# V and K in eight steps of two K tiles instead of four quarters, with the modulation weights in a new order

## What is computed

```python
m = silu(c) @ w_ada + b_ada                    # 9 vectors c; six parts of 2048: shift, scale, gate, twice
h = rms_norm(x, g_pre) * (1.0 + scale) + shift
z = h @ w_in                                   # 2048 -> 4096, columns q | k | v | u
q, k = rotary(q), rotary(k)                    # then differential attention, pooling, output, MLP
```

## Time and profile before

| what | value |
|---|---|
| median of 3 runs | 1501.66 us (1497.08 to 1504.21) |
| the profiled execution | 1498.26 us |
| its span, first to last instruction | 1496.6 us |
| PE busy | 1443.1 us (96%) |
| DVE busy | 798.9 us (53%) |
| ACT busy | 516.9 us (35%) |
| POOL busy | 102.5 us (7%) |
| mean granted TensorE clock | 0.995 |
| moved by DMA | 316.40 MB |

### The profile page before, as it was taken

One profiled execution on the slowest core, in us unless ns is written; L12 is line 12 of the kernel. 1 busy time (PEld: TensorE's weight loads), 2 busy tenths in 40 slices (PEclk: granted clock), 3 DMA queues, 4 the chain that ended last, 5 costly groups with the idle time before them and its releaser, 6 DMA issues.

```text
span 1496.6 us, 26948 instructions
## 1 busy us (share of the span) xinstructions
PE 1443.1 (96%) x10264; PEld 1313.5 (88%) x10264; DVE 798.9 (53%) x1258; ACT 516.9 (35%) x732; POOL 102.5 (7%) x177
## 2 busy tenths in 40 slices
PE   5999999999899998999999999999999999999996
PEld 1677777778688877999998999999999999999996
DVE  2555558846756568665434444334555344445554
ACT  2222244333356445333232333322333332333331
POOL 1000000067410000000000000000000000000002
PEclk9999999999999999999999999999999999999998
DMA  9999988889677787445445544445544444444431
GB/s 367 341 322 325 322 306 311 284 310 347 245 296 251 257 280 240 155 140 168 140 147 199 189 147 162 141 159 184 195 157 147 151 158 141 141 154 154 141 113 71
DMA packets 87880, 316.40 MB, mean 211 GB/s; under 512 B 12176, under 2 KB 12432, under 8 KB 87168
## 3 DMA queue, kind: packets, MB, share of 16 engines
q1 hardware_dynamic: 79200, 287.87, 55.9%
q0 software_dynamic: 5216, 22.51, 4.0%
q10 hardware_dynamic: 3392, 5.01, 1.0%
HBM read 309.56 MB, written 5.80 MB: 211 GB/s over the span
## 4 chain that ended last, share of the span: by engine, by line
PE 83%; DVE 5%; DMA 5%; POOL 2%; ACT 2%; issue 2%; POOLq 1%; SPq 0%; DVEq 0%; ACTq 0%
PE bank L1519 69%; PE bank L1583 7%; DMA raw<-in_stream 3%; PE bank L1481 3%; PE bank L1496 2%; DMA k_pages<-in_kc 1%; DVE w_lo L774 1%; DMA pools_out<-u_s 1%; POOL win L1382 1%; ACT w_hi L389 0%; ACT pair L631 0%; DVE back L978 0%; POOLq L1363 0%; DVE pair L1184 0%; ACT h_hi L635 0%
## 5 line engine op out<-in xcount | busy, mean ns | idle before, releaser
L774 DVE TENSOR_TENSOR w_lo<-raw,w_hi 128x1024 fp32r<-128x1024 f32 x352 | 419.6, 1225 | 121.7 <-ACT w_hi L389 119.8
L389 ACT ACTIVATE w_hi<-raw 128x1024 fp32r<-128x1024 f32 x352 | 361.6, 1054 | 355.9 <-PE bank L1519 232.8
L1519 PE MATMUL bank<-m_hi,w_hi 128*128 128x320 f32 x1280 | 397.4, 310 | 0.6 <-issue 0.6
L1519 PE MATMUL bank<-m_hi,w_lo 128*128 128x320 f32 x1280 | 395.5, 309 | 0.0
L1519 PE MATMUL bank<-m_lo,w_hi 128*128 128x320 f32 x1280 | 395.5, 309 | 0.0
L1519 PE MATMUL bank<-h_hi,w_hi 128*128 128x320 f32 x1216 | 379.2, 312 | 0.0
L1519 PE MATMUL bank<-h_hi,w_lo 128*128 128x320 f32 x1216 | 375.7, 309 | 0.0
L1519 PE MATMUL bank<-h_lo,w_hi 128*128 128x320 f32 x1216 | 375.6, 309 | 0.0
L1519 PEld LDWEIGHTS bank<-m_hi,w_hi 128*128 128x128 f32 x1280 | 240.3, 188 | 14.6 <-issue 14.6
L1519 PEld LDWEIGHTS bank<-h_hi,w_hi 128*128 128x128 f32 x1216 | 228.2, 188 | 24.1 <-issue 24.1
L1519 PEld LDWEIGHTS bank<-m_lo,w_hi 128*128 128x128 f32 x1280 | 240.3, 188 | 0.0
(11 more groups left out here) (234 smaller groups left out, 1093.8 us busy)
## 6 DMA issues: line engine op xcount, KB each, us to landing
raw<-in_stream SPq DMA_DIRECT2D x544, 512.0 KB, 4.9
k_pages<-in_kc POOLq DMA_DIRECT2D x16, 512.0 KB, 9.2
v_pages<-in_vc POOLq DMA_DIRECT2D x16, 512.0 KB, 7.3
x<-in_x_cm ACTq DMA_DIRECT2D x1, 2560.0 KB, 12.1
x<-in_x_cm POOLq DMA_DIRECT2D x1, 2560.0 KB, 11.3
v_out<-v_cm POOLq DMA_DIRECT2D x1, 1280.0 KB, 9.7
k_out<-back POOLq DMA_DIRECT2D x1, 1280.0 KB, 9.8
y_out<-x SPq DMA_DIRECT2D x2, 640.0 KB, 3.0
```

The costliest lines, as they stand in the source:

```text
L389: act.activation(w_hi[2 * (j % 2) + h][:, :], raw[slot][:, h * 1024:(h + 1) * 1024], ACT.Copy).then_inc(hi_ready, 1)
L774: dve.tensor_tensor(w_lo[q][:, :], raw[slot][:, h * 1024:(h + 1) * 1024], w_hi[q][:, :], ALU.subtract).then_inc(slot_used[slot], 1)
L1519: last = pe.matmul(bank[j % 2][:, 0:T], w[q][:, k * P:(k + 1) * P], v[:, 8 * h + k, :], start=(h == 0 and k == 0 and n == 0), stop=(h == 1 ...
```

## The change

**Steps.** V and K are made in eight steps (`SLICES`) of two K tiles. A product chunk now has eight column tiles by two K tiles: one chunk for V and one for K a step. A half has four column tiles, one in each of the four banks, six matmuls each, so a bank comes round once a half. The products stand at places 0, 3, 6, 9 of the 12 (`SLICED`). The number of chunks, of product matmuls and of modulation matmuls is the same; DVE adds 128 tiles of partial sums instead of 64.

**Modulation.** Block n (0 to 7) now has both scale and shift of two K tiles (`MOD_TILES`), so the first product needs block 0 alone: the head has four modulation chunks instead of eight. Block n+1 comes during step n. The prompt's scale and shift are one ACT instruction a K tile (`slice_h`, Identity with scale and bias); POOL's two operations are half as wide.

**Head.** x comes on SP's queue in four pieces ahead of the stream. PE sums the squares before block 0. DVE makes `normed` for eight K tiles before block 0 is added up.

**Q stage.** The four chunks that the head lost are here: 28 chunks, products at 0, 4, 7, 11, 14, 18, 21, 25 (`Q_PLACES`), 20 modulation chunks before a product or in its middle (`Q_BEFORE`, `Q_MIDDLE`).

```diff
-STREAM = 8 + 12 * QUARTERS + 12 * Q_GROUPS + 8 * (U_GROUPS + OUT_GROUPS) + 36 * GROUPS
-DENSE = [2, 5, 8, 11]
-DENSE_ADA = [[0, 1, 3, 4], [6, 7, 9, 10]]
+SLICES = 2 * QUARTERS
+STREAM = 4 + 12 * QUARTERS + 28 + 8 * (U_GROUPS + OUT_GROUPS) + 36 * GROUPS
+SLICED = [0, 3, 6, 9]
+SLICED_ADA = [[1, 2, 4, 5], [7, 8, 10, 11]]
+Q_PLACES = [0, 4, 7, 11, 14, 18, 21, 25]
+Q_ADA = [n for n in range(28) if n not in Q_PLACES]
+Q_BEFORE = [[0, 1, 2], [4], [6, 7], [9], [11], [13, 14], [16, 17], [19]]
+Q_MIDDLE = [[3], [5], [8], [10], [12], [15], [18], []]
+Q_TURN = {0: 9, 2: 10, 4: 11}
+NORMED = [(0, 2), (2, 4), (4, 8), (8, 12), (12, 16)]
...
     @block.sync
     def _(sp):
+        for g in range(4):
+            sp.dma_start(x[:, 4 * g:4 * g + 4, :], x_cm[:, 4 * g:4 * g + 4, :]).then_inc(x_loaded[g], 16)
...
     @block.scalar
-        act.dma_start(x[:, :, :], x_cm).then_inc(x_loaded, 16)
...
+        def slice_h(n):
+            act.wait_ge(gate_done, n + 1)
+            act.wait_ge(normed_s, normed_by(n))
+            act.wait_ge(mod_done, n + 2)
+            for k in range(2):
+                tile = normed[:, 2 * n + k, 0:NP_]
+                act.activation(tile, tile, ACT.Identity, bias=mod[:, n, 2 + k, 0:1], scale=gate[:, 2 * n + k, 0:1]).then_inc(
+                    prompt_mod, 1)
+            act.wait_ge(prompt_mod, 2 * n + 2)
+            act.wait_ge(sample_mod, n + 1)
+            act.activation(h_hi[:, 2 * n:2 * n + 2, :], normed[:, 2 * n:2 * n + 2, :], ACT.Copy).then_inc(h_hi_s, 1)
+
         ada_copy(0, 0, 3)
-        ada_copy(1, 1, 3)
+        hi_half(0, quarter_use(0), SLICED[0], 0, 0)
+        slice_h(0)
+        hi_half(0, quarter_use(0), SLICED[0], 0, 1)
...
+        for n in range(SLICES):
+            second, following = slice_chunks(n)
+            for h in range(2):
+                hi_half(*second, h)
+            ada_copy(n + 1, quarter_use(n // 2), SLICED_ADA[n % 2][3])
+            hi_half(*following, 0)
+            if n + 1 < SLICES:
+                slice_h(n + 1)
+            hi_half(*following, 1)
...
     @block.vector
+        def slice_gate(n):
+            mod_add(n)
+            dve.wait_ge(mod_done, n + 2)
+            dve.scalar_tensor_tensor(gate[:, 2 * n:2 * n + 2, :], mod[:, n, 0:2, :], 1.0,
+                                     gain[:, G_PRE_MIX + 2 * n:G_PRE_MIX + 2 * n + 2].unsqueeze(2).to_broadcast([P, 2, NSEQ]),
                                      ALU.add, ALU.mult).then_inc(gate_done, 1)
...
+        invert_root(0)
+        for first, end in NORMED[:3]:
+            times_rstd(first, end)
+        slice_gate(0)
+        lo_half(0, quarter_use(0), SLICED[0], 0, 0)
+        low_of_h(0)
+        lo_half(0, quarter_use(0), SLICED[0], 0, 1)
...
+        for n in range(SLICES):
+            second, following = slice_chunks(n)
+            for h in range(2):
+                lo_half(*second, h)
+                sum_tiles(n, 0, h)
+            if n + 1 < SLICES:
+                slice_gate(n + 1)
+            else:
+                mod_add(n + 1)
+            lo_half(*following, 0)
+            sum_tiles(n, 1, 0)
+            if n + 1 < SLICES:
+                low_of_h(n + 1)
+            lo_half(*following, 1)
+            sum_tiles(n, 1, 1)
...
     @block.tensor
-        for a in range(3):
-            ada_chunk(0, 0, a, a)
         sum_parts(0)
-        ada_chunk(0, 0, 3, 3)
         mean_of_parts(0)
+        for a in range(4):
+            ada_chunk(0, 0, a, a)
         pe.wait_ge(tables_loaded, 48)
         ada_turn(0)
-        for a in range(4):
-            ada_chunk(1, 1, a, a)
-        ada_turn(1)
...
+            for i in range(2):
+                nb, places = 2 * g + (i + 1), SLICED_ADA[i]
+                ada_chunk(nb, use, places[0], 0)
+                pe.wait_ge(h_ready, 2 * g + (i + 1))
+                slice_tiles(i, 0, 0, range(4))
+                ada_chunk(nb, use, places[1], 1)
+                ada_chunk(nb, use, places[2], 2)
+                slice_tiles(i, 0, 1, range(2))
+                ada_chunk(nb, use, places[3], 3)
+                slice_tiles(i, 0, 1, range(2, 4))
+                ada_turn(nb)
+                slice_tiles(i, 1, 0, range(4))
+                slice_tiles(i, 1, 1, range(4))
```

More of the change, by code:

```diff
@@ L445, in ada_fill @@
         def ada_fill(f):
-            done = fill_ada(f)[1]
-            if done is not None and done < PARTED:
-                ada_copy(done, fill(f)[1], fill(f)[2] - 1)
+            if f in Q_TURN:
+                ada_copy(Q_TURN[f], *[chunk[1:3] for part in fill_ada(f) for chunk in part if chunk[0] == Q_TURN[f]][-1])
         def evac_fill(f):
@@ new lines, in times_rstd @@
+        def times_rstd(first, end):
+            dve.tensor_tensor(normed[:, first:end, :], x[:, first:end, :],
+                              rstd[:, :].unsqueeze(1).to_broadcast([P, end - first, T]), ALU.mult).then_inc(normed_s, 1)
+        invert_root(0)
+        for first, end in NORMED[:3]:
[4 more added lines that the diff above has]
+        lo_half(0, quarter_use(0), SLICED[0], 0, 1)
+        for first, end in NORMED[3:]:
+            times_rstd(first, end)
@@ new lines, in _, with sum_tiles @@
+        dve.wait_ge(normed_s, len(NORMED))
+        dve.wait_ge(sums_zeroed, 2)
+        def sum_tiles(n, jj, h):
+            half = 4 * n + 2 * jj + h
+            for i in range(4):
+                if i < 3:
+                    dve.wait_ge(first_done, 3 * half + i + 1)
+                else:
+                    dve.wait_ge(half_free, half + 5)
+                tile = (v_cm, k_cm)[jj][:, 4 * h + i, :]
+                dve.tensor_tensor(tile, QUARTER_BANKS[i][:, 0:T], tile, ALU.add).then_inc(bank_free[i], 1)
@@ L909, in mod_fill @@
         def mod_fill(f):
[L910 to L912 removed]
+            if f in Q_TURN:
+                mod_add(Q_TURN[f])
             if f == 15:
@@ new lines, in slice_tiles @@
+            def slice_tiles(i, jj, h, tiles):
+                j = 2 * i + jj
+                slot, u = use_of(use, SLICED[j])
+                q = 2 * (j % 2) + h
+                pe.wait_ge(slot_used[slot], 2 * u + (3 + h))
+                for b in tiles:
+                    pe.wait_ge(bank_free[b], 8 * g + (2 * j + h + 1))
+                    for k in range(2):
+                        for n, (w, v) in enumerate(((w_hi, h_hi), (w_hi, h_lo), (w_lo, h_hi))):
+                            last = pe.matmul(QUARTER_BANKS[b][:, 0:T], w[q][:, (2 * b + k) * P:(2 * b + k + 1) * P],
+                                             v[:, ds(4 * g + (2 * i + k), 1), :].rearrange("p a t -> p (a t)"),
+                                             start=(k == 0 and n == 0), stop=(k == 1 and n == 2))
+                    last.then_inc(first_done if b < 3 else half_free, 1)
```

274 lines of the change are left out of this document (91 added, 183 removed).

## The result

The changed kernel takes **1521.05 us** (median of 4 runs, 1519.9 to 1526.4), against 1499.76 for the kernel before in the same comparison. The ratio is 1.0147, 95% interval 1.0126 to 1.0168: slower by 21 us, where the prediction had 1489.5 and faster.

The account below looks back on a forecast made before the run. Transfers and a four-engine chain bound the head, PE the stages behind. Head -13.7, moved work +5.4, seams -1.5, Q stage -2.4, V/K loop and clock 0 sum to -12.2: 1489.5 us from 1501.66, range 1483 to 1499.

Parts of the forecast that it names:

- Head, -13.7: Head: first product at 30.0 us, 13.7 us earlier, after block 0's last half lands at 23.0.
- rival 1: V/K steps: place 4's slot comes free too late, PE waits 2.4 us in each of eight steps, 1508; chance 0.08.
- Moved work +5.4: Behind the first product: five modulation chunks at 0.98 us and one turn of 0.5 us move there, +5.4 us.
- seams -1.5: V/K: three changes between product and modulation a step instead of four, at 0.19 us each, -1.5 us.
- V/K loop 0: V/K steps of 19.06 us: 64 more sums, 27 us, lie in DVE's idle time and no bank waits, 0.
- rivals 2 and 3: V/K banks: PE waits 1 us a step, 1497.5, chance 0.10; late head transfers: first product at 33, 1492.5, chance 0.06.
- Q stage, -2.4: Q stage: half of PE's 4.7 us of waits for the rotated q goes, -2.4 us, as product slots come free earlier.
- Rival 4: Q stage starves: 28 chunks, 20 leaning on low halves' slots, bring 5 us of new waits, 1496.9; chance 0.06.
- Clock, 0: Behind the first product: the same 1.3 us loss at PE's 1.2 GHz as before, 0, bounds -1.3 and +1.3.

Follow-up runs that it names:

- the early split: Second half of each Q product split ahead of the softmax on ACT and DVE: 1496.95 us on the changed kernel, 1499.63 on the kernel before.
- two versions three apart: Changed kernel, Q products three places apart, without and with early split: leftover chunks behind the last product 1495.99 and 1495.90 us, all in front 1506.00 and 1505.06.
- the one 3 or 5 apart: Changed kernel with Q products at places 0, 5, 8, 11, 14, 17, 22, 27: 1497.86 us, with the early split 1495.55.
- the run with places 3 or 5 apart and the head's late half: Changed kernel, Q products 3 or 5 places apart, first V/K product's second half split before h_hi and h_lo: 1498.30 us.
- the use order with the head's late half: Changed kernel, Q products streamed in PE's order of use, first V/K product's second half split before h is made: 1501.21 us.

## Why the prediction was wrong

- **Head, -13.7.** Measured -14.7. The last half came at 21.73 and not 23.0; from there to the first product I had 7.0 us and it took 7.2. POOL was held by the low half as argued: 1.34 beside it, 0.47 alone, in the rows above. POOL ended 0.3 us behind the low half that began first. This agrees with the rule of the Trainium skill that the prediction cited (SBUF — State Buffer, "SBUF: two separate sides").
- **First step.** Not in my sum: from its first product to that of the second step 22.3 us (28.94 to 51.25) instead of 19.06, nearly all of it the late chunk at place 4 that rival 1 describes, once instead of eight times. +3.2.
- **Moved work +5.4, seams -1.5, V/K loop 0.** Right to within 0.6 us: the other seven steps were 19.15 apart (19.06 forecast). Up to the first Q product the parts are the head -14.7, the first step +3.2, the two moved chunks that lie in V/K +2.0, the seams -1.5, the steps +0.6 and the clock behind the first product -1.3 (below): -11.7, and the lead there is 11.8. My own terms give -13.7 + 2.0 - 1.5 = -13.2 for this place, so 1.4 us were missing already; that it is no more is in part luck, since the saved clock and the longer lead of the head cancel some of the late chunk. PE was busy throughout steps 2 to 8, with no wait for a bank: the 64 additional sums are hidden, rivals 2 and 3 did not happen.
- **Q stage, -2.4.** This step failed. It measured +34.95 - 3.4 for the chunks and turn moved there = +31.5. Its own subject came out in part: the waits before the scores, 4.7 us before, are 3.0. The step asked when the slot of each *product* comes free, said that those at 18 and 25 "wait for the low half of the product before and are no better", and stopped there. Two things were missing. The product at 11 waits in the same way, four places behind the one at 7. And nobody asked which modulation chunks are themselves the next tenant of a late product's slot (15 and 22) or are queued *behind* a chunk that waits for one: places 12, 13, 16, 19, 20, 23, 24, 26 and 27. PE uses all of these before the product they stand behind. SP's wait is harmless only if all behind it is used later.
- **Rival 4** named the right stage and even the low halves that lag behind PE, but said that 20 chunks lean on their slots, where seven do (places 4, 8, 11, 15, 18, 22 and 25), looked for the trouble in the amount moved, and priced it at 5 us of new waits with a chance of 0.06. The waits for the stream alone add up to 19 us between 190 and 295, and the low clock behind them to about 14 more.
- **Clock, 0.** Wrong twice. In the head the granted clock was 0.50 from 25.5 to 28.9 us, where PE made one modulation chunk in 3.16 us, and 1.00 from the first product on; so the 1.3 us that the kernel before loses behind its first product were saved. And as a consequence of the waits it was 0.92 in the Q stage, where it had been 1.00.

Two theories of the study fell as well. That two kinds of wait explained the whole remainder (A's first range) did not hold. And that the late second low half costs by itself was not borne out: the early split gave nothing on the kernel before, 0.1 and 0.9 us on two versions three apart, 2.3 on the one 3 or 5 apart, where the chain shows another product waiting behind it.

## What to carry to other kernels

With a ring of slots fed by one queue in order, check for every transfer not only when its slot comes free, but also what stands behind it and is needed sooner; put the stream in the order of use first, and make it differ only for a reason. A tenant that releases late (here a product behind a softmax, four places back) should have nothing urgent at or behind its successor's place. When work is added to such a ring, look at the stage that receives it at least as closely as at the stage it leaves: the 12 us gained in front were bought with 35 behind.

## What was unexpected

A wait of PE cost nearly twice its idle time here: 17.6 us of idle time came with about 14 more of busy time, most of it work at 1.2 GHz by the estimate above. The stream was never short of bandwidth: in the stage that starved it moved 261 GB/s on average against 299 before, and 420 in the 4 us after a release, more than the 373 of the head. The later stages, which the change doesn't touch, differed between profiled executions by up to 5 us from pages to end: 1180.9 in the run with places 3 or 5 apart and the head's late half, 1181.0 in the changed kernel, 1182.2 before, 1185.9 in the use order with the head's late half. The difference is busy time of PE (1154.2 against 1160.6) at a granted clock of 1.00 and 0.99, and not idle time; why the clock differs is open. A few us between two profiles are therefore no finding by themselves.
